# Turning the first tile of a sample early, between the outputs of a dense pass

## The reference, cut to what matters

```python
merged = g_a * (attn @ lp['w_oa']) + g_b * (hy @ lp['w_ob'])
x = x + gate1 * (merged @ lp['w_out'])
h2 = _rmsnorm(x, lp['norm_ffn']) * (1 + scale2) + shift2
x = x + gate2 * _peer(h2, lp['peer_wq'], lp['peer_keys'], lp['peer_u'], lp['peer_v'])
...
def _peer(h, wq, sub_keys, u_tab, v_tab):
    q = (xt @ wq).reshape(T, P_HEADS, 2, KEY_HALF)
    s = jnp.einsum('thpk,hpnk->thpn', q, sub_keys).astype(jnp.float32)
    s1, i1 = lax.top_k(s[:, :, 0], P_TOPK)
    s2, i2 = lax.top_k(s[:, :, 1], P_TOPK)
    cand = (s1[..., :, None] + s2[..., None, :]).reshape(T, P_HEADS, P_TOPK * P_TOPK)
    top, pos = lax.top_k(cand, P_TOPK)
    g = jax.nn.softmax(top, axis=-1).astype(h.dtype)
    ...
        u = jnp.take(u_tab, i_i, axis=0)
        a = jax.nn.gelu(jnp.einsum('td,thkd->thk', x_i, u))
        return jnp.einsum('thk,thkd->td', a * g_i, jnp.take(v_tab, i_i, axis=0))
```

## Time and profile before

| what | value |
|---|---|
| median of 3 runs | 4868.67 us (4866.35 to 4880.0) |
| span of the profiled execution | 4858.6 us |
| busy | TensorE 3814.1, VectorE 3260.8, GpSimd 1793.3, ScalarE 1557.8 us |
| mean granted clock of TensorE | 0.915 of full speed |
| DMA | 1602.62 MB, mean 330 GB/s |
| last merged channel of the sample in layer 0 | 1107 us from the start of the span |
| first gather of the sample, layer 0 and 1 | 1227.39 and 3468.39 us |

### The profile page before, as it was taken

How to read it: one execution, slowest core, us unless ns; L and a number is a source line. 1 busy time by engine, 2 the same in 40 slices (tenths; PEclk the granted TensorE clock), 3 DMA queues, 4 the chain that set the end, 5 groups by cost and what they waited for, 6 DMA issues and landing times.

```text
span 4858.6 us, 42229 instructions
## 1 busy us (share of the span) xinstructions
PE 3814.1 (79%) x12642; PEld 2042.6 (42%) x12642; DVE 3260.8 (67%) x7651; ACT 1557.8 (32%) x4562; POOL 1793.3 (37%) x1515
## 2 busy tenths in 40 slices
PE   7987788797798766767877679799699777777776
PEld 4546464445454223323543346445555332322222
DVE  2323788858867986666567778876877876755555
ACT  2321241101234344434333323110233444444444
POOL 2330132333234434455344323224233444444443
PEclk8889889898899889898989889899799999999999
DMA  7565376766799989999999767766689999999998
GB/s 269 203 225 202 136 272 256 272 242 260 314 372 384 391 332 422 398 411 385 395 416 421 295 231 267 289 230 272 248 352 359 412 405 415 418 414 421 421 421 347
DMA packets 231264, 1602.62 MB, mean 330 GB/s; under 512 B 27558, under 2 KB 29906, under 8 KB 42876
## 3 DMA queue, kind: packets, MB, share of 16 engines
q0 software_dynamic: 198016, 1395.87, 72.4%
q1 hardware_dynamic: 33020, 204.06, 10.8%
HBM read 1588.52 MB, written 11.30 MB: 329 GB/s over the span
## 4 chain that ended last, share of the span: by engine, by line
PE 38%; DMA 28%; DVE 21%; issue 5%; ACT 5%; POOL 2%; SPq 0%; ACTq 0%; DVEq 0%; POOLq 0%
DMA sb_arena<-in_peer_uv,sb_idx 15%; PE ps L1133 14%; DMA sb_gbufs<-in_peer_uv,sb_idx 10%; PE ps L1029 7%; DVE sb_gbufs L1929 4%; PE ps L1070 4%; DVE sb_arena L1929 3%; DVE sb_eacc L1952 2%; PE ps L717 2%; PE ps L744 2%; PE ps L887 1%; DMA sb_ring<-in_w_oab 1%; DVE sb_arena L1915 1%; ACT sb_small L1393 1%; POOL sb_gbufs L2172 1%
## 5 line engine op out<-in xcount | busy, mean ns | idle before, releaser
L2172 POOL DMA_INDIRECT sb_gbufs<-in_peer_uv,sb_idx x768 | 981.9, 1279 | 1783.7 <-PE ps L1133 758.4
L1133 PE MATMUL ps<-sb_gbufs,sb_dge 128*128 128x512 f32 x1856 | 912.3, 641 | 281.5 <-ACT sb_dge L1413 274.0
L1133 PE MATMUL ps<-sb_arena,sb_dge 128*128 128x512 f32 x1856 | 902.4, 636 | 267.2 <-ACT sb_dge L1413 267.0
L2172 POOL DMA_INDIRECT sb_arena<-in_peer_uv,sb_idx x512 | 610.3, 1192 | 789.4 <-PE ps L1133 691.7
L1929 DVE CUSTOM_DVE_ANT_0 sb_gbufs<-sb_gbufs,sb_keep 128x1024 f32<-128x1024 f32 x512 | 625.6, 1235 | 355.7 <-DMA sb_gbufs<-in_peer_uv,sb_idx 352.5
L1929 DVE CUSTOM_DVE_ANT_0 sb_arena<-sb_arena,sb_keep 128x1024 f32<-128x1024 f32 x512 | 622.1, 1229 | 327.0 <-DMA sb_arena<-in_peer_uv,sb_idx 325.0
L1133 PEld LDWEIGHTS ps<-sb_gbufs,sb_dge 128*128 128x128 f32 x1856 | 363.1, 204 | 793.0 <-issue 392.3
L1133 PEld LDWEIGHTS ps<-sb_arena,sb_dge 128*128 128x128 f32 x1856 | 360.8, 202 | 777.2 <-issue 390.5
L1390 ACT ACTIVATE sb_small<-sb_small 128x2 f32<-128x2 f32 x512 | 104.1, 203 | 1516.3 <-DVE sb_small L1929 1491.1
L1952 DVE SCALAR_TENSOR_TENSOR sb_eacc<-sb_gbufs,sb_small,sb_eacc 128x1024 f32<-128x1024 f32 x299 | 387.3, 1295 | 7.8 <-DVE sb_small L1962 0.3
L1397 ACT ACTIVATE sb_small<-sb_small 128x1 f32<-128x1 f32 x1024 | 340.6, 379 | 49.6 <-ACT sb_small L1393 2.2
(11 more groups left out here) (272 smaller groups left out, 4276.7 us busy)
## 6 DMA issues: line engine op xcount, KB each, us to landing
sb_ring<-in_w_wq SPq DMA_DIRECT2D x48, 1024.0 KB
sb_keep<-in_w_ada POOLq DMA_DIRECT2D x52, 512.0 KB, 6.1
sb_ring<-in_w_hy SPq DMA_DIRECT2D x24, 1024.0 KB
sb_ring<-in_w_ga SPq DMA_DIRECT2D x16, 1024.0 KB
sb_ring<-in_w_gb SPq DMA_DIRECT2D x16, 1024.0 KB
sb_ring<-in_w_oab SPq DMA_DIRECT2D x16, 1024.0 KB
sb_ring<-in_w_out SPq DMA_DIRECT2D x14, 1024.0 KB
sb_gbufs<-in_peer_uv,sb_idx POOLq DMA_INDIRECT x768
```

Source lines behind the costliest of these rows:

```text
L1133: q = pe.matmul(ps[:, c, :], dge[:, b, :], gbuf[b][:, D + c * 512:D + c * 512 + 512], start=(h == 0 and i == 0), stop=(h == HALVES - 1 and ...
L2172: nc.gpsimd.indirect_dma_start(out=gbuf[b], out_offset=None, in_=I["peer_uv"], in_offset=bass.IndirectOffsetOnAxis(ap=idx[:, col:col + 1], ...
```

## The change

The order of the end of the sample's dense pass is now a table, `tail_points`, which all engines follow. Tiles 1 and 2 get their outputs, tile 1 is turned by itself, and its first two queries stand between the outputs of tiles 3 and 4. Tiles 2 to 4 are turned at a point of their own, behind all queries of tile 1, where the token steps already run. The numbers of hT's columns 384 to 511 hold the queries and the best values of tile 1 meanwhile (`qh0`, `best_of_first`), so that ScalarE's copies of tiles 2 to 4 wait for tile 1's last scores and for the gates of its last route. The first query weights get a place of their own in the arena. The square of a tile is written over its norm's place. The prompt's units are spread over the changed paces.

```diff
+def tail_points(g):
+    if not g.latent:
+        return [("out", q // 4, q % 4) for q in range(4 * g.nt)] + [("turn", 0, 0)] + [("query", 0, i) for i in range(NHP + 1)]
+    out = [[("out", j, i) for i in range(4)] for j in range(4)]
+    first = [("query", 0, i) for i in range(NHP + 1)]
+    return out[0] + out[1] + [("turn", 0, 0)] + out[2][0:2] + first[0:1] + out[2][2:4] + first[1:2] + out[3] + first[2:] + \
+        [("turn", 1, 0)] + [("query", 1, i) for i in range(NHP + 1)]
...
+    def turn_bank(self, p, c):
+        return 2 + c % 2 if p else self.lo(c)
...
-        return at + (...) + [3.5] * (4 * nt) + [20] + ([4.0] * 17 + [7.0] * 17 if self.latent else [7.5 * k + 1] * 17)
+        return at + (...) + \
+            [{"out": 3.5, "turn": 4 if self.latent else 20, "query": 7.5 * k + 1 if not self.latent else (4.0, 7.0, 0, 0)[p[1]]}[p[0]] for p in tail_points(self)]
...
-            out += [((d, kind, i), 2048, None, free("qh_ps", NHP * p + 2 * i + 2)) for i in range(8)]
+            out += [((d, kind, i), 2048, g.o["wq0"] if g.latent and p == 0 and i == 0 else None, free("qh_ps", NHP * p + 2 * i + 2)) for i in range(8)]
...
-        wq = len(pace) - 2 * (NHP + 1)
-        end = sum(pace[:wq]) / sum(pace)
+        names = tail_points(GR[1])
+        wq, last_before = (len(pace) - len(names) + names.index(("query", 0, i)) for i in (4, 2))
+        end = sum(pace[:last_before]) / sum(pace)
...
-        second, between = NHP, [f"R{j}" for j in (2, 3, 4) for _ in range(PIECES)]
+        second, between = NHP + 1, [f"R{j}" for j in (2, 3, 4) for _ in range(PIECES)]
...
-                if m == first and between:
+                if first - 1 <= m <= first and between:
                     order.append(between.pop(0))
...
             def dense(d):                                  # TensorE
+                def turn(p):
+                    j0, j1 = g.parts[p]
+                    pe.wait_ge(*at("h2", j1))
+                    for c in range(KD):
+                        b = g.turn_bank(p, c)
+                        claim(b, *at("hT2", KD * p + c + 1))
+                        for j in range(j0, j1):
+                            m = pe.transpose(ps[:, b, (j - j0) * 128:(j - j0) * 128 + 128], h2_of(g, j)[:, c * 128:c * 128 + 128], ident[:, :])
+                        m.then_inc(s["tr2"], 1)
...
             def dense(d):                                  # ScalarE
+                def turned_again(p):
+                    j0, j1 = g.parts[p]
+                    if p:
+                        act.wait_ge(*at("sc_ps", NHP))
+                        act.wait_ge(Z["gw1"], 4 * layer + 4)
+                    for c in range(KD):
+                        act.wait_ge(*at("tr2", KD * p + c + 1))
+                        act.activation(v.hT[:, c, j0 * 128:j1 * 128], ps[:, g.turn_bank(p, c), 0:(j1 - j0) * 128], ACT.Copy).then_inc(s["hT2"], 1)
+
+                for what, p, i in tail_points(g):
+                    if what == "out" and i == 3:
+                        act.wait_ge(*at("xadd", outputs(g).index((p, i)) + 1))
+                        junk = h2_of(g, p) if g.latent else v.junk2
+                        act.activation(junk, x[:, g.t0 + p, :], ACT.Square, accum_out=st[:, p:p + 1]).then_inc(s["ss2"], 1)
...
             def dense(d):                                  # VectorE
+                places_of_norm = {("out", j + 1, 1): j for j in range(nt - 1)}
+                places_of_norm["query", 0, 2] = nt - 1
```

149 lines of the change are left out of this document (74 added, 75 removed).

## The result

| | median us | runs | ratio to before, 95% interval |
|---|---|---|---|
| before | 4870.0 (4866.35 to 4880.0) | 5 | |
| after | 4894.33 (4888.45 to 4897.06) | 5 | 1.0047 (1.0032 to 1.0062) |

The time rose by 24.3 us; 33 were forecast, on top of the median 4868.67, so 4902 against 4894. In this result every execution of the changed kernel has its span beside its time: 4897.06 with 4895.2, 4894.33 with 4892.5. So 1.9 us lie around a span, not 10.1 as the prediction took it. The execution that the profile before shows was a short one (span 4858.6, so some 4860.5 us), and the 10.1 us between its span and the median are mostly the scatter between executions. A comparison of the two traces alone would give +36.6 us, 12 more than the runs.

A forecast was written before the change was run, and what follows sets the result against it. No engine bounds the whole: VectorE bounds the dense pass's end, TensorE the token steps with queries, DMA the stretch behind them. Terms -1 + 16 + 2 + 0 + 16 = +33 on 4868.67 gave 4902 us, range 4872 to 4922.

The forecast's parts named there:

- (a): From the last merged channel to the first sample gather: about -1 us in layer 0, 0 in layer 1.
- The rival in which the seam gains: Before the first gather, tile 2's square comes early enough: -8 to -10 us per layer, 4884 us; chance 0.18.
- The units' price: Three expert units leave layer 0's stretch behind the last merged channel, -4 us, and cost 1 us in earlier stages.
- (b): Turning tiles 2 to 4 between the fourth and fifth sample token steps (V4, V5) delays later steps: +16 us per layer.
- (c): Routing of tiles 2 to 4 starts one token step later, with two pieces doubled: +2 us in layer 0.
- (d): First query weights, in a place of their own, arrive before the outputs end; 1 MB more transferred: 0 us.
- the first gather over 8 us earlier: Sign of a wrong forecast at the first sample gather, which was expected within 5 us of its old place in both layers.
- TensorE's hole was the price: TensorE's idle stretch before the old turning sets the time; turning tile 1 early shortens it: -15.4 us, 4853; chance 0.09.

The follow-up runs named there:

- gates-first kernel: Changed kernel with tile 1's last route ahead of the fifth token step's dot products, tiles 2 to 4 turned behind the fourth, old routing pieces: 4870.92 us, 1.0003.
- the second set: The changed kernel word for word, timed again in 6 runs against the kernel before: 4891.24 us, ratio 1.0044.

## Why the prediction was right, and where it was not

**(a), the seam: right, with the wait in its place.** The turning of tile 1 ends at 1141.7 and output 9 is awaited for 7.53 us; 8.5 were worked out from the square of tile 2. The pair of outputs takes 9.70 us in the changed kernel, at a granted clock of 0.74, and 7.07 at 1.00: 2.6 us for the clock, 2.2 in the prediction. The rival in which the seam gains needed the square earlier; it starts 49.0 us behind the last merged product, and 46.5 before. The sum of this step was -1 in layer 0, with -4 and +1 for moved units in it, and 0 in layer 1; from the last merged product to the first gather it is -0.9 and -1.5. In layer 0 the terms hold in part: the three units left 2.5 us (119.2 against 121.7 with the units alone) for the 4 foretold, the waits for ScalarE's tanh fell from 6.0 to 2.3 us (-4.3 foretold), and those for gathered data rose from 5.9 to 7.3 where -1 was taken. In layer 1 the level sum is luck: the units alone cost this seam 3.7 us, and the new end won 5.2 of them back, neither of which the prediction had.

**The units' price: this is the step that failed.** It took "3 x 1.3 = 4 us less" at the seam and 1 us for the same units ahead of it, and cost the order of all other units at nothing. Measured alone, the new places bring layer 0's dense pass 12 to 13 us, 10 of them ahead of the seam, and cost layer 1's 5, most of it in the seam (by the traces), together a ratio of 0.9985, 7 us; in layer 0 alone 0.9964, 17 us. The 5.3 us that the changed kernel loses ahead of layer 1's seam were not foretold either, and the units' places do not explain them. The prediction counts 40 and 37 units from ahead of the last channel's own units, the section on the change 31 and 29 from behind them; both counts are right. The spread is computed from the sum of all paces, so a change of the list's end changes how many units stand ahead of 81 of the first 107 points in layer 0 and of 85 in layer 1, and the prediction read only the tail of that order.

**(b), the turning: right in mechanism and size.** V5 was put 15.1 us late against the first gather, V7 14.0, V22 15.2, V23 17.2. It is 1314.07 - 1211.34 - (1313.06 - 1227.39) = 17.1, then 14.2 and 16.9, and V1 to V23 is longer by 17.5 and 18.7. What was carried on was 16 a layer; it is 17.5 and 18.7. The third group of transposes waited 14.50 us (14 foretold), released by ScalarE's copy and this by the gates. The 2 us by which V5 is later than foretold are the gates: 97.7 us behind the first gather, 95.8 before. The 1 us that was added because V5 would come cold has no run behind it: V5 took 7.03 us, at a granted clock of 1.00 in 1314 to 1321, and it was the last 18 transposes ahead of it that had the 0.51 of 1310 to 1314. The experiments split the price: some 6.5 us is V5 standing in the queue, 3.7 is one query step more ahead of V23, about 1 goes with the gates, and some 7 us a layer are left in the gates-first kernel (297 against 290).

**(c), the routing: right in layer 0, missed in layer 1.** +2 was taken in layer 0, where +0.7 is within the scatter. In layer 1 nothing was taken and it is +5.7; the doubled piece falls on step 42 there, and some 4 of these are its price. The diff showed it: `first - 1` is 42, a multiple of three.

**(d): right.** What the queries wait for their weights (L1070 before, L1105 after, both passes of both layers) is 4.9 us on both pages.

**The sum.** By traces -2.6 - 13.5 + 17.5 + 1.1 + 3.9 + 18.7 + 5.7 - 0.1 = +30.7; the forecast was -1 + 16 + 2 + 0 + 16 = +33. That the two agree is luck. Errors of opposite signs took each other away: -12.6 ahead of layer 0's seam, where +1 stood, and -2.6 ahead of E, against +5.3 ahead of layer 1's seam, +5.7 behind its V23, and the turnings, +4.2 more than 32. By the runs it is +24.3 and, in the second set, +21.4. The remaining 6 to 9 us are a matter of which executions were traced: the one of before lay 10 us under the median. The range, 4872 to 4922, was laid out for other mishaps and held. One sign of being wrong, the first gather over 8 us earlier, came true in layer 0, and it pointed at the right thing: time that the prediction had not priced, ahead of the seam.

*TensorE's hole was the price* fell as the prediction said it would: the turning no longer stands behind that hole, and the seam is level, since VectorE's work and waits there sum up to the same.

## What to carry to other kernels

Before work is moved behind a wait, ask what stands behind the waiting instruction in the same queue: here 5 us of transposes, with a wait of 14.5 us among them, held back a token step that had been ready for 13.7 us, and another order in that queue took 6.5 us off each layer. When an order is computed from a sum over all entries, price every entry that moves, not those near the edit: the side effect in layer 0, 17 us by the runs, was as large as a turning's price, and alone it made the fastest kernel of the study. And cut traces at a count that both kernels share (here the gathers), with two traces of each, before any difference of a few us is given a cause. Where the change moves the counted thing itself, cut at another engine's points too: in layer 1 two kernels agreed in a length of 715 us and differed by 5 in both its halves.

## What was not expected of the hardware

The scatter of one and the same kernel is 4854.62 to 4883.67 us in 12 runs, 0.6%, yet the stretches that TensorE or VectorE set repeat to 0.1 us: V9 to V23 is 173.5 us in both traces of before, in both layers, and 177.2 in those of after. What scatters is where DMA is full or data is awaited: V89 to V97 of layer 0, at a DMA share of 0.98, took 105.3, 108.2, 111.6 and 104.8 us in the four traces. And a gap in the gathers outlasts its cause a little: two pieces of 5.7 us on VectorE left GpSimd without a gather to issue for 12.51 us, where one left 6.17, and V41 to V49 was 6 us longer.
